# A hybrid diffusion trunk on eight cores: weights streamed in another order, units of work woven by counts, and query sums of squares by an accumulating VectorE operation

## The reference

```
z = h @ w_in                      # u (512), cq (384), ckv (256), krope (32)
y_pool = multi_scale_pool(u)      # windows 2, 4, 8, 16, then a 128x128 product per group
q = rms_norm(rms_norm(cq) @ w_uq) # 8 heads of 96, the last 32 rotated for latent tokens
k, v from rms_norm(ckv) @ w_ukv   # keys normalised, with the shared krope part
y = concat(y_pool, softmax(q k) v) @ w_out
```

## Time and profile before

| | us |
|---|---|
| median of 3 runs (1257.90 to 1291.38) | 1259.85 |
| the profiled execution | 1259.46 |
| its span on the slowest core (core 5; cores from 1248.7) | 1258.4 |
| TensorE busy, share of the span | 1137.0, 90% |
| VectorE, ScalarE, GpSimd busy | 480.3, 429.5, 227.8 |
| chain that ended last: TensorE, VectorE, DMA | 76%, 7%, 6% |

### The profile page before, as it was taken

How to read it: one execution, slowest core, us unless ns; L and a number is a source line. 1 busy time by engine, 2 the same in 40 slices (tenths; PEclk the granted TensorE clock), 3 DMA queues, 4 the chain that set the end, 5 groups by cost and what they waited for, 6 DMA issues and landing times.

```text
span 1258.4 us, 17871 instructions; the slowest of 8 cores (1248.7 to 1258.4 us)
## 1 busy us (share of the span) xinstructions
PE 1137.0 (90%) x6857; PEld 547.9 (44%) x6857; DVE 480.3 (38%) x814; ACT 429.5 (34%) x669; POOL 227.8 (18%) x347
## 2 busy tenths in 40 slices
PE   2477678797889899999999999998899999999998
PEld 1233455554544344444444444444344444444443
DVE  0355673634136211152252253565622225125133
ACT  2455466665745511101101156543651110110100
POOL 3311452533213200000000022224310000000000
PEclk9988997868799899999999999998999999999999
DMA  9960318778991425225224206003533321410013
GB/s 187 239 110 1 59 30 141 112 118 130 155 167 36 67 38 92 39 35 84 34 34 84 51 1 109 1 1 49 98 55 67 68 35 34 84 17 1 1 76 126
DMA packets 24977, 90.04 MB, mean 72 GB/s; under 512 B 3392, under 2 KB 3776, under 8 KB 24128
## 3 DMA queue, kind: packets, MB, share of 16 engines
q0 software_dynamic: 21312, 77.10, 36.8%
q1 hardware_dynamic: 3584, 11.80, 2.8%
HBM read 153.85 MB, written 6.88 MB: 128 GB/s over the span
## 4 chain that ended last, share of the span: by engine, by line
PE 76%; DVE 7%; DMA 6%; ACT 5%; POOL 3%; issue 3%; POOLq 0%; ACTq 0%; DVEq 0%
PE pb L230 74%; DMA wslot<-w_in_u 3%; DMA wslot<-ada_w 3%; ACT pt L247 2%; DVE xtmp L268 2%; PE pb L228 2%; DVE kT L274 1%; POOL qs L251 1%; DVE xb L268 1%; DVE qf L274 1%; POOL qr L251 1%; ACT hy L247 0%; ACT xsq L247 0%; POOL qt L251 0%; DVE utok L251 0%
## 5 line engine op out<-in xcount | busy, mean ns | idle before, releaser
L230 PE MATMUL pb<-hb,wslotx 128*128 128x512 bf16 x1440 | 319.9, 379 | 0.0
L247 ACT ACTIVATE sg<-pb 128x512 f32<-128x512 f32 x132 | 78.7, 596 | 472.0 <-PE pb L230 472.0
L251 DVE TENSOR_TENSOR apart<-pb,sg 128x512 bf16<-128x512 f32 x132 | 91.3, 691 | 369.0 <-PE pb L230 346.2
L230 PEld LDWEIGHTS pb<-hb,wslotx 128*128 128x128 bf16 x1440 | 140.8, 98 | 170.0 <-issue 0.3
L268 DVE SCALAR_TENSOR_TENSOR xb<-pb,mod,xb 128x512 f32<-128x512 f32 x192 | 143.6, 749 | 143.1 <-PE pb L230 143.1
L230 PE MATMUL pb<-hb,wslot 128*128 128x512 bf16 x864 | 197.6, 385 | 0.0
L230 PE MATMUL pb<-apart,wslot 128*128 128x512 bf16 x768 | 167.1, 379 | 0.0
L247 ACT ACTIVATE pt<-pb,rk 128x1024 bf16<-128x1024 f32 (+1 forms) x128 | 118.9, 953 | 58.0 <-PE pb L230 57.2
L230 PEld LDWEIGHTS pb<-hb,wslot 128*128 128x128 bf16 x864 | 85.6, 99 | 104.9 <-issue 5.7
L230 PEld LDWEIGHTS pb<-apart,wslot 128*128 128x128 bf16 x768 | 75.1, 98 | 90.2
L230 PE MATMUL pb<-hy,wslot 128*128 128x512 bf16 (+1 forms) x336 | 82.4, 397 | 4.7 <-ACT hy L247 4.5
(11 more groups left out here) (130 smaller groups left out, 953.8 us busy)
## 6 DMA issues: line engine op xcount, KB each, us to landing
wslot<-ada_w POOLq DMA_DIRECT2D x48, 512.0 KB, 10.1
wslot<-ffn_wd POOLq DMA_DIRECT2D x16, 512.0 KB, 9.9
wslotx<-ffn_wu POOLq DMA_DIRECT2D x14, 512.0 KB, 10.6
wslotx<-ffn_wg POOLq DMA_DIRECT2D x12, 512.0 KB, 18.9
y<-xb SPq DMA_DIRECT2D x12, 512.0 KB, 2.7
wslot<-ffn_wg POOLq DMA_DIRECT2D x10, 512.0 KB, 7.4
xb<-x_in POOLq DMA_DIRECT2D x4, 1024.0 KB, 41.7
wslot<-ffn_wu POOLq DMA_DIRECT2D x8, 512.0 KB, 7.5
```

The lines of the kernel that those rows point to most:

```text
L230: return self.op("pe", lambda g: g.matmul(out, lhsT, rhs, start=start, stop=stop), [lhsT, rhs], [out], inc=inc)
L247: return self.op("act", lambda g: g.activation(out=out, in_=in_, func=func, bias=bias, scale=scale), reads, [out])
L251: return self.op(e, lambda g: g.tensor_tensor(out=out, in0=in0, in1=in1, op=op), [in0, in1], [out])
```

## The change

- The stream's list: twelve adaLN pieces (8 to 19) now stand right behind the projection's weights, before `uq0`, `uq1` and `ukv` (before: `ukv`, `uq0`, `uq1`, then all pieces). Eleven slots instead of ten before the feed-forward part, seven instead of eight after it; the three slots given up are now those of `in_kv`, `in_q0` and `in_q1`. The third block of x is issued after the third adaLN piece, not the second.
- `together` replaces the weaving by costs: for every part of the main generator a fixed count of steps of each filler. In the projection of block 0 the norm of block 1 (24 steps in 10 parts); in that of block 1 the norm of block 2 (24), the pooling of block 0 (9, bank 6) and adaLN pieces (5, bank 6); in that of block 2 adaLN pieces (7, bank 6). In the first preparation (18) pooling (18, bank 6 alone) and adaLN pieces (4, bank 7). In the attention a pair's preparation goes at 18 steps in 25 and the pieces left are spread evenly over 108 of the 112 steps.
- `qkv` goes through its units in one order: query and key or value units in turn. Key sums and reciprocal roots are put off by two ticks.
- The sum of squares of a query unit: four VectorE `scalar_tensor_tensor` operations of 96 elements with `accum_out`, one per token tile and head, instead of one multiply on POOL and one reduction on VectorE.
- Tiles: the best-fitting gap instead of the first, two `rs` tiles in the norm instead of three (block 2 uses block 0's), `ckr_f` dropped earlier.

```diff
-        addr = gaps[-1][1] - nbytes if high else gaps[0][0]
+        addr = gaps[-1][1] - nbytes if high else min(gaps, key=lambda g: (g[1] - g[0], g[0]))[0]
...
-        slots = [new("wslot%d" % i, [128, 2048], BF16, high=(i >= 7)) for i in range(10)]
+        slots = [new("wslot%d" % i, [128, 2048], BF16, high=(i >= 8)) for i in range(11)]
...
         ent("in_u1", w_in_u[1], 4, 512)
-        ent("ukv", w_ukv, 2, 1024)
+        ent_ada(8, 20)
         ent("uq0", w_uq[:, 0:2, :], 2, 768)
         ent("uq1", w_uq[:, 2:3, :], 1, 768)
-        ent_ada(8, 48)
+        ent("ukv", w_ukv, 2, 1024)
+        ent_ada(20, 48)
...
-        W.retire.update((7, 8, 9))
+        W.retire.update((8, 9, 10))
...
-                self.rs = [new("xrs%d" % i, [128, 512], F32) for i in range(3)]
+                self.rs = [new("xrs%d" % i, [128, 512], F32) for i in range(2)]
+                self.rs.append(self.rs[0])
...
             ada_piece()
-            if k == 1:
+            if k == 2:
                 load_x("pool", 2)
...
+        def ada_gen():
+            k0 = ada_state["done"]
+            for k in range(k0, 50):
+                if k - 2 >= k0:
+                    W.done(("ada", k - 2))
+                if k < 48:
+                    ada_piece(pool=AB, keep=True)
+                yield 0.4
+        AB = (6,)
+        ada = ada_gen()
+        def together(main, n, parts):
+            for i, _ in enumerate(main):
+                for g, k in parts:
+                    for _ in range((i + 1) * k // n - i * k // n):
+                        next(g, None)
         for b in range(3):
             drain(norms[b])
-            fill = collections.deque()
+            parts = []
             if b < 2:
-                fill.append(norms[b + 1])
+                parts.append((norms[b + 1], 24))
+            if b == 1:
+                parts.append((pooling([0], (6,), 0, lambda o, i, sc: P.ts("dve", o, i, sc, None, ALU.mult)), 9))
             if b > 0:
-                fill.append(pooling([b - 1] if b == 1 else [], (6,), 1.3, lambda o, i, sc: P.ts("dve", o, i, sc, None, ALU.mult)))
-            weave_in(inproj(b), fill)
+                parts.append((ada, 5 if b == 1 else 7))
+            together(inproj(b), 10, parts)
...
-            def reduce(ss, u, qs):
-                P.op("dve", lambda g: g.reduce_sum(out=ss[:, 4 * u:4 * u + 4], in_=qs[:], axis=AX.X), [qs[:]], [ss[:, 4 * u:4 * u + 4]])
+            def square_sum(ss, u, qf, qs):
+                for i in range(4):
+                    acc = ss[:, 4 * u + i:4 * u + i + 1]
+                    P.op("dve", lambda g: g.scalar_tensor_tensor(out=qs[:, i, :], in0=qf[:, i, :], scalar=1.0, in1=qf[:, i, :],
+                                                                 op0=ALU.mult, op1=ALU.mult, accum_out=acc),
+                         [qf[:, i, :]], [qs[:, i, :], acc])
...
-                    P.tt("pool", qs[:], qf[:], qf[:], ALU.mult)
-                    later(1, functools.partial(reduce, ss, u, qs))
+                later(1, functools.partial(square_sum, ss, u, qf, qs))
...
+            order = [("q", 0, 0), ("k", 3), ("q", 0, 1), ("v", 3), ("q", 1, 0), ("k", 0), ("q", 1, 1), ("v", 0),
+                     ("q", 2, 0), ("k", 1), ("q", 2, 1), ("v", 1), ("k", 2), ("v", 2)]
+            for kind, *arg in order:
+                {"q": q_unit, "k": k_unit, "v": v_unit}[kind](*arg)
                 yield 0.5
                 tick()
+            later(2, krstd)
...
-        q0 = qkv(0, (0, 1, 2, 3, 4, 5))
-        weave(q0, collections.deque([pooling([1, 2], FB, 0.5, lambda o, i, sc: P.act(o, i, AF.Copy, scale=sc))]), flush=True)
+        pool12 = pooling([1, 2], (6,), 0, lambda o, i, sc: P.act(o, i, AF.Copy, scale=sc))
+        AB = (7,)
+        together(qkv(0, (0, 1, 2, 3, 4, 5)), 18, [(pool12, 18), (ada, 4)])
+        drain(pool12)
+        AB = FB
...
-        for i, idle in enumerate(attention(before)):
-            debt += idle
-            while debt > 0:
...
-            if i % 5 in (1, 3):
+        left = 50 - ada_state["done"]
+        for i, _ in enumerate(attention(before)):
+            n = i % 28
+            for k in range((n + 1) * 18 // 25 - n * 18 // 25):
+                next(nxt[0], None)
+            if (i + 1) * left // 108 > i * left // 108:
                 next(ada, None)
```

More of the change, by code:

```diff
@@ L825, in build @@
         key_sums(3)
+        drop(ckr_f)
         def inproj(b):
@@ new lines, in square_sum, with q_unit @@
+            def square_sum(ss, u, qf, qs):
[4 more added lines that the diff above has]
+                         [qf[:, i, :]], [qs[:, i, :], acc])
+            def q_unit(b, u):
+                if u == 0:
+                    qst[b] = (ssr.next(), ssr.next(), [])
+                ss, sr, qts = qst[b]
+                ps = P.bank(banks)
+                for i in range(2):
+                    t = 4 * b + 2 * u + i
+                    P.mmg(ps[:, i * 192:(i + 1) * 192], [(cqn[:, kc, t * 128:(t + 1) * 128], wuq[kc][:, p * 192:(p + 1) * 192]) for kc in range(3)])
+                qf = qfr.next()
+                qs = qsr.next()
+                qt = qtr.next()
+                qts.append((qf, qt))
+                P.cp("dve", qf[:].rearrange("p a d -> p (a d)"), ps[:, 0:384])
+                later(1, functools.partial(square_sum, ss, u, qf, qs))
+                if u == 1:
+                    later(2, functools.partial(rnorm, ss, sr))
+                    for v in range(2):
+                        later(3 + v, functools.partial(rotate, b, v, qts[v][0], qts[v][1], sr))
+                    later(6, functools.partial(turn, b, [x[1] for x in qts]))
@@ L1077, in qkv, with sums @@
             ksb = new("ksb", [128, 16, 2], F32)
-            pend = None
-            def sums():
-                kb, sq = pend
+            def sums(kb, sq):
                 ps = P.bank(banks)
@@ L1086, in sums, with k_unit @@
                 P.tt("dve", ksb[:, kb * 4:kb * 4 + 4, :], ps[:, 0:8].rearrange("p (a b) -> p a b", b=2), k_bc, ALU.add)
[L1088 removed]
+            def k_unit(kb):
                 ps = P.bank(banks)
[L1090 to L1091 removed]
+                P.mmg(ps[:], [(wukv[:, kc, p * 256:p * 256 + 128], ckvn[kb][:, kc, :]) for kc in range(2)])
                 sq = sqk.next()
@@ L1095, in qkv, with v_unit, krstd @@
                     P.cp("act" if p == 0 and hl == 1 else "dve", kT[0:64, hl, blk(kb)], ps[hl * 64:hl * 64 + 64, :])
-                yield 0.43
-                tick()
+                later(2, functools.partial(sums, kb, sq))
+            def v_unit(kb):
                 ps = P.bank(banks)
                 for i in range(4):
-                    rv = [wukv[:, kc, p * 256 + 128:p * 256 + 256] for kc in range(2)]
-                    P.mmg(ps[:, i * 128:(i + 1) * 128], [(ckvn[kb][:, kc, i * 128:(i + 1) * 128], rv[kc]) for kc in range(2)])
+                    P.mmg(ps[:, i * 128:(i + 1) * 128],
+                          [(ckvn[kb][:, kc, i * 128:(i + 1) * 128], wukv[:, kc, p * 256 + 128:p * 256 + 256]) for kc in range(2)])
                 P.cp("dve", V[:, kb * 4:kb * 4 + 4, :, 0:64], ps[:].rearrange("p (t h d) -> p t h d", t=4, h=2))
+            def krstd():
+                P.act(ksb[:], ksb[:], AF.Ln, bias=epsc[:, 3:4])
+                P.act(rk[:], ksb[:], AF.Exp, scale=-0.5)
+                drop(ksb)
+            qst = {}
+            order = [("q", 0, 0), ("k", 3), ("q", 0, 1), ("v", 3), ("q", 1, 0), ("k", 0), ("q", 1, 1), ("v", 0),
+                     ("q", 2, 0), ("k", 1), ("q", 2, 1), ("v", 1), ("k", 2), ("v", 2)]
+            for kind, *arg in order:
+                {"q": q_unit, "k": k_unit, "v": v_unit}[kind](*arg)
                 yield 0.5
                 tick()
[L1105 to L1112, removed]
+            later(2, krstd)
             while lag:
@@ L1115, in qkv @@
                 tick()
[L1117 to L1124, removed]
         SD = [P.pb[:, 0:1024], P.pb[:, 1024:2048]]
@@ L1207, in attention @@
                 todo.popleft()[1]()
-        q0 = qkv(0, (0, 1, 2, 3, 4, 5))
-        weave(q0, collections.deque([pooling([1, 2], FB, 0.5, lambda o, i, sc: P.act(o, i, AF.Copy, scale=sc))]), flush=True)
+        pool12 = pooling([1, 2], (6,), 0, lambda o, i, sc: P.act(o, i, AF.Copy, scale=sc))
[3 more added lines that the diff above has]
+        AB = FB
         drop(*pbr.t)
+        ytk = Ring([new("ytk%d" % i, [128, 12, 128], BF16) for i in range(2)])
         kvq.append(new_kvq(1))
-        ytk = Ring([new("ytk%d" % i, [128, 12, 128], BF16) for i in range(2)])
-        ada = ada_gen()
         nxt = [iter(())]
@@ L1241, in build @@
         N = Norm()
-        W.more([new("wslotx%d" % i, [128, 2048], BF16) for i in range(8)])
+        W.more([new("wslotx%d" % i, [128, 2048], BF16) for i in range(7)])
         norms = {}
@@ L1253, in build @@
         drop(*hy)
-        W.more([new("wslotx%d" % i, [128, 2048], BF16) for i in range(8, 8)])
+        W.more([new("wslotx%d" % i, [128, 2048], BF16) for i in range(7, 7)])
```

43 lines of the change are left out of this document (2 added, 41 removed).

## The result

| | before | after |
|---|---|---|
| median of six runs each, us | 1258.76 | 1279.80 (1265.44 to 1449.94) |
| ratio, 95% interval | | 1.0103 [1.0055, 1.0150] |
| profiled execution, us | 1259.46 | 1271.79 |
| the same kernel timed again (eight and eleven runs), us | 1261.54 | 1267.08 |
| ratio of that comparison | | 1.0047 [1.0029, 1.0065] |

A forecast was written before the change was run, and what follows sets the result against it. Transfers set the pace up to 84 us, no engine is full in the attention, and TensorE covers the tail; projection +10, preparation -2 and attention -15 sum to -7, so 1252 us, bounds 1240 to 1264, range 1226 to 1280.

The forecast's parts named there:

- The wait for `band`: Projection, block 1: band lands at 92.2 us, an 11 us wait; what stands behind it runs 6.6 us later.
- Five adaLN pieces stand directly behind a pooling step and share bank 6 with it ... +5: Projection, block 1: each piece waits 0 to 1.72 us for VectorE to empty the bank; +5 us (0 to +8.6).
- block 3's term: Projection: norm steps finish a block earlier, saving 4 us of idle time and half the clock's loss; -6.5 us (-3 to -9).
- twelve pieces at 0.4 us: Projection: twelve adaLN pieces on TensorE, 0.57 us each, overlapping with neighbours, so 0.4 each; +5 us (0 to +7).
- Pooling now has one bank instead of two; the pairs of steps depend on each other anyhow, so nothing: First pair's preparation: one pooling bank costs nothing, and +4 us if ScalarE and VectorE are late.
- VectorE's relief: First pair's preparation: VectorE's 4.1 us of waiting for GpSimd go; its extra accumulating work puts +1.5 us on the path.
- Rival 4: Accumulating operations hold VectorE in preparation and attention, from about 0.45 us each; 1273 to 1285 us and over; chance 0.12.
- the +3 for VectorE: Attention: of VectorE's +2.9 us per pair, a third lies on the path; +3 us (0 to +10).
- The clock I leave at its share: Attention: the granted clock was left at its share, with 71 us counted at the lower level before.
- rival 1: Attention: clock stays at 2.4 GHz, 71 us at 1.11 instead of 1.49, -18; 1234 us, possibly 1218; chance 0.20.
- The waits of TensorE for kT: Attention: these waits, 6.3 + 4.1 us, are halved with fewer units a step; -5 us (-10 to +3).
- Rivals 2 and 3: 2: attention's clock stays low, 1272 us, chance 0.12; 3: pieces only change places, attention shortens by 5, 1262 us, chance 0.14.

The follow-up runs named there:

- e2: Changed kernel with adaLN pieces ahead of the norm and pooling steps in each part of the projection; 1257.10 us (before 1259.48).
- e6: Changed kernel with all forty adaLN pieces left in the attention, new stream order otherwise; 1253.15 us (before 1259.78).
- e11: Changed kernel with all 40 adaLN pieces left in the attention, band issued early, preparation's pooling on banks 6 and 7; 1242.29 us, 0.9838 against before.
- e12: e7 with only the seven adaLN pieces of block 2 moved, none in block 1, 33 in the attention; 1246.07 us, 0.9855 against before.
- e5: Kernel before with only the accumulating VectorE operations in place of GpSimd's multiply and VectorE's reduction; 1260.58 us, 1.0021 against before.
- e4: Changed kernel with the former squares, one GpSimd multiply and one VectorE reduction per query unit; 1269.77 us (before 1259.48).
- e13: e11 with query units ahead of key and value units in every pair; 1246.23 us (before 1257.92).
- e7: Changed kernel with band early, adaLN pieces ahead of norm and pooling, preparation's pooling on banks 6 and 7 and no piece there; 1240.25 us (before 1259.78).

## Why the prediction was wrong

Two steps failed, one in the projection and one in the preparation. The attention came out better than forecast, and made up for all but 5 us of what they cost.

**The projection: the first step that failed.** Forecast +10, measured +21 (107.9 against 86.8).
- The wait for `band` was right: landing forecast at 92.2, and the product that needs it starts at 92.46. What stands behind it is 92.46 - 83.70 - 1.9 = 6.9 us later, against 6.6. The wait is 8.9 us and not 11, since TensorE itself came later, after 2.75 us for `hy` that the sum had not. w_in_u's wait is gone, as said, and so is block 3's 3.29 us.
- **"Five adaLN pieces stand directly behind a pooling step and share bank 6 with it ... +5"** is the mis-sized term: it measured 12.35 us, beyond its upper bound of 8.6. The bound took 1.72 us a piece from a row of the kernel before, in which one `utok` alone stood ahead of the copying (`hy`, VectorE of core 5, the two lines below). Here the copying behind the last three pieces stands behind the norm of block 2 and behind `utok`, `cqn` or the krope steps, with a wait for ScalarE among them. e2 takes the pieces from behind pooling, and 10 us go.
- The clock after the waits was costed only in block 3's term, 2.5 us of whose gain it was to take back. Matmuls at half speed after 92.46 cost (3.57 - 1.89) + (1.49 - 0.81) + (1.02 - 0.63) = 2.8 us, and those after 115 and 126 us (eight in 2.97, seven in 3.19, eight in 2.31) about 3 more.
- Block 3's own gain was 8.3 us, against 6.5: without pieces it takes 21.1 us (e6, e11) and not 29.4. The changed kernel's 25.6 us hold its seven pieces (2.0 us, e11 to e12) and the 2.73 us of the fifth piece's wait as well.

With twelve pieces at 0.4 us, as forecast, the terms are 6.9 + 12.35 + 4.8 + 5.8 - 8.3 = 21.6, near the 21 measured.

```profile
98.75 0.69 DVE L251 TENSOR_TENSOR utok<-pb,utok 128x512 bf16<-128x512 f32 x1 [1.90 <-ACT utok L273]
99.36 0.74 DVE L259 TENSOR_SCALAR hy<-pb,vecs 128x512 bf16<-128x512 f32 x1
```

**The preparation: the second step that failed.** Forecast -2, measured +8, beyond the upper bound of +4. "Pooling now has one bank instead of two; the pairs of steps depend on each other anyhow, so nothing" was wrong: the product and its copying out of the bank now take turns with the next step's first product, and the pooling product waits 6.5 us for ScalarE, where the main wait had been for VectorE. The lower clock there (0.75; e11 has 0.93) goes with the gaps. The second bank is worth 5.6 us (e6 to e11) and block 2's last piece 1.8. The other 0.5 us are left with neither: e11 takes 30.8 us, and before it was 30.3. The forecast had VectorE's relief at 2.6 of the 30.2 us; the new squares alone, in e5, gave 0.8.

**The operation.** Forecast 256 ns, measured 260, which is in part luck: the forecast went by elements alone, and the mean holds operations of 250 and of 449 ns, by what GpSimd was doing. For VectorE's time a pair, +2.9 us was forecast and 4.96 - 3.3 = +1.7 measured, with the read of the accumulator and within the bounds of 0.6 to 9.8; the forecast added up full lengths, which overlap. Each has an accumulator read of 82 ns behind it. That it is an instruction of its own is what the Trainium skill says (VectorE: DVE Perf Modes, Two Vector instructions with no wait between them), and the trace agrees; my estimate of 163 ns for it was twice too high. On the other rule, that VectorE and GpSimd contend when both need the shared ports (SBUF — State Buffer, Who interferes with whom), the trace agrees: `qt` takes 410 ns, and 1050 where GpSimd's multiply had started first. `qt`'s mean falls from 627 ns before to 442 after and 417 in e5, without the multiply; in e4, with the multiply in the new order of units, it is 467. Rival 4 needed 0.45 us an operation; with its read one holds VectorE for 4.96 / 24 = 0.21 us, and by e4 and e5 the time stands.

**The attention.** Forecast -15, measured -24, so the direction was right and the size 9 us short. The pieces gave 6.7 against -5, and the +3 for VectorE did not come (e4, with the former squares, takes 0.7 us more and not less). What makes the other 4 to 5 us is open. "The clock I leave at its share" failed: the share fell from 58 us at the lower level (twice what the cores' median clocks 0.86, 0.84, 0.83 and 0.86 lack of 1.00, times each pair's length; the forecast's 71 us are core 5's alone) to 26 (0.94, 0.92, 0.92, 0.91 when run again) or 35 (the first profile). At the price of rival 1, 32 us x (1 - 1.11/1.49) = 8 us at most. So rival 1's clock came in part. That the clock caused the gain is argued, not shown: the two profiles of the changed kernel differ by 9 us in that sum and take the same 167.2 us, and e11 and e13 stand at 42 and 44 us and differ by 6.5 us. The waits of TensorE for kT, 6.3 + 4.1 us before and halved in the forecast, fell by a third: the transposes' part is gone, and that of the 128-row matmuls is 7.2. Waits of the attention, core 0, 194.3 to 361.9 us:

```profile
PE pb L230 <- DVE kT L274: 7.2, 6, 1.6
```

The forecast's sum, with +21 for +10, +8 for -2 and -24 for -15, comes to +5. Rivals 2 and 3 did not come: the clock of the attention rose, and it shortened by far more than 5 us.

## What to carry to other kernels

A matmul that shares a PSUM bank with another group of work waits until another engine has copied the bank's content out, and for all that stands ahead of that copy in the engine's order: 1.29 us where VectorE was free here, up to 3.68 where it was not. So price the sharing with the queue as it will be, and not with a row in which that engine was free. A small load that the critical path needs goes ahead of every prefetch in its queue, as slots that are free early put megabytes in front of it. Filler work that pays in one stage can cost as much in the stages that take it in: e7's twelve moved pieces save 9.9 us and cost 9.7, and e11, which left the pieces where they were, has as short a sum of stages.

## What the runs showed of the hardware

- An accumulating `scalar_tensor_tensor` over 96 f32 elements takes about 250 ns and is followed by a read of its accumulator of 82 ns. The next one starts 0.17 us after it started, and 24 of them with their reads, in groups of four, hold VectorE for 4.96 us.
- A `tensor_tensor` of 128x256 with two SBUF inputs takes 410 ns, and 1050 where GpSimd's multiply of 128x384, also from SBUF, had started first. The accumulating operation goes from about 250 to 449 ns in the changed kernel, and to 501 in e5, in the same way.
- The granted clock of the same work differed with the waits in it: block 1, 194 and 195 TensorE instructions, had 0.76 in the changed kernel and 0.90 in e7, which waits less.
